# Low parts of 40 first-layer weight tiles made by adding transfers instead of GpSimd subtractions

## The reference, cut to what matters

```
h = rms_norm(x, norm_g)
q, k, v, gate = split(h @ w_in, 4)          # w_in is 2048 x 8192
q, k = partial_rope(q), partial_rope(k)     # 16 heads of 128
w = softmax(q1 k1) - lam * softmax(q2 k2)   # 8 pairs
o = rms_norm(w @ v, subln_g) * 0.8          # then o * silu(gate)
x = x + o @ w_out                           # w_out is 2048 x 2048
```

## Time and profile before

| | |
|---|---|
| median of 3 runs | 2815.59 us (2815.26 to 2817.22) |
| the profiled execution: its time, as the profile gives it | 2815.378 us |
| its span | 2815.4 us |
| PE busy | 2783.0 us, 99% |
| DVE, ACT, POOL busy | 1270.5, 996.7, 1170.6 us |
| DMA, mean rate | 88 GB/s |

### The profile page before, as it was taken

One profiled execution on the slowest core, in us unless ns is written; L12 is line 12 of the kernel. 1 busy time (PEld: TensorE's weight loads), 2 busy tenths in 40 slices (PEclk: granted clock), 3 DMA queues, 4 the chain that ended last, 5 costly groups with the idle time before them and its releaser, 6 DMA issues.

```text
span 2815.4 us, 41127 instructions
## 1 busy us (share of the span) xinstructions
PE 2783.0 (99%) x16886; PEld 2422.6 (86%) x16886; DVE 1270.5 (45%) x2182; ACT 996.7 (35%) x1466; POOL 1170.6 (42%) x895
## 2 busy tenths in 40 slices
PE   8999999999999999999999999999999999999997
PEld 8999999999999999777877778888788877887776
DVE  6333333334343358343434352744434334455646
ACT  5323232222323245344233354542323333234444
POOL 3343334334343434333434337444444334445443
PEclk9999999999999999999999999999999999999999
DMA  5122222222222222222222234222222222222221
GB/s 194 64 88 76 90 76 76 90 76 76 90 76 76 91 69 90 90 76 75 83 82 75 90 112 150 90 75 90 90 83 82 90 91 75 90 83 90 90 90 76
DMA packets 37115, 247.53 MB, mean 88 GB/s; under 512 B 4112, under 2 KB 4416, under 8 KB 8640
## 3 DMA queue, kind: packets, MB, share of 16 engines
q1 hardware_dynamic: 34992, 239.37, 24.0%
q10 hardware_dynamic: 1936, 5.53, 0.5%
HBM read 240.69 MB, written 4.19 MB: 87 GB/s over the span
## 4 chain that ended last, share of the span: by engine, by line
PE 91%; DVE 4%; ACT 2%; DMA 1%; POOL 1%; DVEq 1%; issue 0%; ACTq 0%; SPq 0%
PE pj L337 20%; PE pj L344 20%; PE pj L341 20%; PE pj L400 3%; PE pj L404 3%; PE pj L402 3%; PE pj L1184 2%; PE pj L1186 2%; PE pj L1185 2%; PE pa L586 1%; PE pa L549 1%; PE pa L1087 1%; POOL wl L2426 1%; DMA raw<-in_stream 1%; PE pj L1099 1%; PE pa L1523 1%
## 5 line engine op out<-in xcount | busy, mean ns | idle before, releaser
L2426 POOL TENSOR_TENSOR wl<-raw,wh 128x512 fp32r<-128x512 f32 x872 | 1158.9, 1360 | 1613.2 <-ACT wh L279 1613.2
L337 PE MATMUL pj<-xh,wh 128*128 128x264 f32 (+2 forms) x3728 | 1080.4, 336 | 2.9 <-POOL wl L2426 1.4
L341 PE MATMUL pj<-xl,wh 128*128 128x264 f32 (+2 forms) x3728 | 1044.7, 326 | 0.0
L344 PE MATMUL pj<-xh,wl 128*128 128x264 f32 (+2 forms) x3712 | 1040.9, 327 | 0.0
L279 ACT ACTIVATE wh<-raw 128x2048 fp32r<-128x2048 f32 x219 | 419.3, 1914 | 944.2 <-PE pj L344 594.8
L337 PEld LDWEIGHTS pj<-xh,wh 128*128 128x128 f32 x3728 | 633.8, 188 | 74.4 <-issue 15.2
L341 PEld LDWEIGHTS pj<-xl,wh 128*128 128x128 f32 x3728 | 631.0, 188 | 62.0 <-issue 7.2
L344 PEld LDWEIGHTS pj<-xh,wl 128*128 128x128 f32 x3712 | 628.0, 188 | 59.4
L429 DVE TENSOR_TENSOR acc<-pj,acc 128x528 f32<-128x528 f32 (+1 forms) x192 | 134.2, 699 | 126.7 <-PE pj L404 125.6
L400 PE MATMUL pj<-oh,wh 128*128 128x264 f32 (+1 forms) x608 | 167.2, 326 | 3.5 <-DVE ol L931 1.5
L404 PE MATMUL pj<-oh,wl 128*128 128x264 f32 (+1 forms) x608 | 165.1, 323 | 0.0
(11 more groups left out here) (331 smaller groups left out, 2804.5 us busy)
## 6 DMA issues: line engine op xcount, KB each, us to landing
raw<-in_stream SPq DMA_DIRECT2D x219, 1024.0 KB, 4.8
acc<-in_x SPq DMA_DIRECT2D x8, 528.0 KB, 8.8
raw<-in_stream SPq DMA_DIRECT2D x8, 256.0 KB, 8.1
arena<-in_mem ACTq DMA_DIRECT2D x2, 1024.0 KB, 6.1
out_y<-arena SPq DMA_DIRECT2D x4, 512.0 KB, 2.9
out_y<-arena ACTq DMA_DIRECT2D x3, 512.0 KB, 4.5
out_y<-arena SPq DMA_DIRECT2D x1, 384.0 KB, 4.4
cos<-in_cos_a SPq DMA_DIRECT2D x1, 264.0 KB, 11.9
```

What stands on the lines that cost most here:

```text
L337: pe.matmul(pj[:, pu, b, 0:m], whk, xh[:, k, a:a + m], start=(k == 0), stop=False)
L341: ins = pe.matmul(pj[:, pu, b, 0:m], whk, xl[:, k, a:a + m], start=False, stop=(both and k == KD - 1))
L344: ins = pe.matmul(pj[:, pu, b, 0:m], wlk, xh[:, k, a:a + m], start=False, stop=(k == KD - 1))
L2426: pool.tensor_tensor(wl[:, j, at], raw[:, j, at], wh[:, j, at].bitcast(F32), ALU.subtract).then_inc(s_part if c < LO_PARTS - 1 else s_lo, 1)
```

## The change

For the 40 tiles 22 to 61, ACT writes wl = -round(raw) with one more instruction of the full 128 x 2048 just ahead of the one that writes wh. POOL then issues two transfers of 128 x 1024 float32 (512 KB each) which read the tile in HBM once more and add it to what stands in `wl`, so that raw - round(raw) is left there. POOL waits for each transfer, raises `s_part` twice after the first and once after the second, and then waits for `s_hi` and raises `s_lo`. The other tiles are as before.

```
+LO_BY_DMA = range(22, 62)
 ...
             act.wait_ge(s_out, used + 1)
+            if t in LO_BY_DMA:
+                act.activation(wl[:, par_t, :], raw[:, par_t, :], ACT.Copy, scale=-1.0).then_inc(s_neg, 1)
             act.activation(wh[:, par_t, :], raw[:, par_t, :], ACT.Copy).then_inc(s_hi, 1)
 ...
+            def lo_by_dma(t, j):
+                n = t - LO_BY_DMA[0]
+                pool.drain()
+                pool.wait_ge(s_neg, n + 1)
+                half = WCOLS // 2
+                for c in range(2):
+                    at = slice(c * half, (c + 1) * half)
+                    pool.dma_start(wl[:, j, at], dram["stream"][t][:, at], accum_op=ALU.add).then_inc(s_low[c], 16)
+                pool.wait_ge(s_low[0], 16 * (n + 1))
+                pool.sem_inc(s_part, 2)
+                pool.wait_ge(s_low[1], 16 * (n + 1))
+                pool.sem_inc(s_part, 1)
+                pool.wait_ge(s_hi, t + 1)
+                pool.sem_inc(s_lo, 1)
 ...
+                    elif pair * 2 + j in LO_BY_DMA:
+                        lo_by_dma(pair * 2 + j, j)
```

More of the change, by code:

```diff
@@ L153, in build @@
         s_out = sem("s_out")
+        s_neg = sem("s_neg")
+        s_low = [sem("s_low0"), sem("s_low1")]
         s_evac = sem("s_evac")
```

## The result

The changed kernel takes 2820.67 us (median of 14 runs, 2819.75 to 2824.03), the kernel before 2816.11 us (14 runs, 2815.26 to 2817.32). The ratio is 1.0016, 95% interval 1.0009 to 1.0024: 4.6 us slower, clear of its own interval and still inside the 0.2% that the prediction called no change. The forecast was 2818.9 us, range 2815 to 2848.

A forecast was written before the change was run, and what follows sets the result against it. TensorE, busy for 516.18 of 516.50 us in pairs 2 to 5, was taken as the limit. Removed work 0 to 0.3 us, delayed exponentials 3.3, other terms 0: 2818.9 us against the median, range 2815 to 2848.

The forecast's parts named there:

- What bounds the kernel; removed work is worth 0 to 0.3 us.: Pairs 2 to 5: TensorE's pace is the limit, so removing POOL's 210 us of subtractions gives back at most 0.3 us.
- The high part 1.92 us later costs nothing.: ACT's high part comes 1.92 us later behind the negated copy; tile 31 still has 8 us to spare, cost nothing.
- The exponentials behind the pair.: Stages 3 and 4, pairs 2 to 5: the longer ACT pair delays exponentials, PE waits; 3.3 us taken.
- The widening of the margin in pairs 4 and 5: Narrower slack there may widen to pair 2's once POOL's subtractions are gone: 3.0 instead of 3.5 us, 3.3 taken.
- The second sigmoid is covered.: A pair's second sigmoid starts 1.92 us later; VectorE's 2.45 us wait for PE behind it covers this, cost nothing.
- rival 3: VectorE, freed of POOL's interference, swallows the ACT delay, leaving 0 to -0.3 us: 2815.3 us; chance 0.06.
- The adding transfers land 8.7 us after the copy, cost 0.: Both halves land 8.7 us after the negated copy; w_out tiles allow 9.5 and 10.1 us, so no wait.
- a cover of 0.8 us: At the first w_out tile, the margin between the expected landing at 8.7 us and the 9.5 us allowed.
- Rival 1: Additions land late at the 8 w_out tiles, from 9.5 us on: 2824.5, 2836 or 2849 us; chance 0.27.
- Rival 2: Above 11.7 us per landing, transfers bound every tile: up to 128 us more, 2944 us; chance 0.11, shared with another rival.
- The total: 2815.4 us of the profiled execution plus 3.3 gives 2818.7; against the median 2818.9 us, +0.12%, counted as no change.

The follow-up runs named there:

- E4: The change for 24 tiles only, without the w_out tiles and those ahead of exponentials in stages 3 and 4: 2816.25 us, ratio 1.0000 to the kernel before.
- E10: Changed kernel with one 1 MB adding transfer per tile, and in stages 3 and 4 the negated copy behind the first following exponential: 2816.07 us, ratio 0.9998.
- E1: Changed kernel without adding transfers: ScalarE makes the negated copy, GpSimd's four subtractions then overwrite it as before: 2819.53 us, ratio 1.0012.
- E3: The change for 32 tiles, without the two per pair of heads ahead of exponentials (stages 3 and 4): 2818.26 us, ratio 1.0007.
- E5: Changed kernel with plain transfers in place of the adding ones, so wl holds the whole weight: 2818.79 us, ratio 1.0011.
- E6: Changed kernel with one adding transfer of 1 MB per tile in place of two of 512 KB: 2819.48 us, ratio 1.0013.
- E8: Changed kernel where SP loads the next tile without waiting for the low part, so beside the adding transfers: 2841.15 us, ratio 1.0088.
- E7: Changed kernel where ScalarE writes the high part first and the negated copy second: 2832.43 us, ratio 1.0059.

## Why the prediction was right, and where it was not

- *What bounds the kernel; removed work is worth 0 to 0.3 us.* Right. 134 us less of POOL and 16 us less of VectorE moved nothing (E4 for 24 tiles, E10 for all 40). The cap of 0.3 us from the earlier trace rows held in every experiment: none was measurably faster.
- *The high part 1.92 us later costs nothing.* Right: the list of waits for pairs 2 to 5 has none of PE for it.
- *The exponentials behind the pair.* Right in place and mechanism (E1, E3, E10), 3.3 us predicted, 2.8 measured. In stage 4 the term was 2.7, measured 2.2. In stage 3 I had 0.8 and found 0.6: a wait of 0.11 us was worked out from rows that left 0.12 us over. Both have the same error: I took the second instruction of the pair as 1.9 us behind the first one's end, and the following exponential's start after that. But ScalarE's instructions overlap by 0.1 us, as 352.24, 354.06 and 355.86 above show: the next one starts 3.62 us after the pair does, not 3.83. With 3.62 the working gives waits of 0.41 us in stage 4 of pair 2 and 0.26 in stage 3 of pair 5, where 0.52 and 0.39 were measured, so a further 0.1 us at each place goes the other way; its cause is open. The widening of the margin in pairs 4 and 5, for which I had taken 0.2 us off, did not come: pair 5's stage 3 is longer by 0.39 us in E1 and by 0.39 in the changed kernel.
- *The second sigmoid is covered.* Right. VectorE's steps there even became shorter, as rival 3 had it; its timeline after, which answers to the earlier trace rows:

```profile
390.92 0.71 DVE L927 TENSOR_TENSOR arena<-arena 128x528 f32<-128x528 f32 x1
391.73 1.33 DVE L936 TENSOR_TENSOR ol<-arena,oh 128x528 fp32r<-128x528 f32 x2
```

  0.71 us in place of 1.64 for the same instruction: beside POOL's subtractions it had taken more than twice as long. The Trainium skill's rule ("SBUF — State Buffer", Who interferes with whom), that two SBUF inputs on VectorE contend with a GpSimd instruction that reads SBUF, agrees. Against the kernel before it is worth nothing: no tile of E4 is shorter. But it keeps the added copy from costing more, since with the subtractions left in place (E1) PE waits 0.13 us per pair for a VectorE instruction beside them, and without them (E5) it does not.
- *The adding transfers land 8.7 us after the copy, cost 0.* This step failed: the landing was mis-sized (9.2 us in the median), and a cover of 0.8 us was held against one number where the landings scatter. Term by term: the lead, from the end of the copy to the first packet, is 1.9 us and not the 0.9 read off SP's load. POOL needs 0.3 us to begin and 0.87 for the first issue, and the first packet comes 0.7 after that. The moving is 7.0 us, as predicted, but by luck: I had doubled the 3.5 us of a single load (its row shows 24 busy slices and not 26, but its packets do take 3.5, from 393.33 to 396.81 us), and a single adding transfer moves in 6.1 (E6). The two halves take 0.9 longer than one transfer, where I had put the second issue at 0.5. A packet takes 1.9 times as long as a plain one (E5), so doubling was nearly right as such. With 0.3 us for the landing, 1.9 + 6.1 + 0.9 + 0.3 makes the measured 9.2 us. Against 9.5 and 10.1 us of room even that median fits; but tiles scatter from 8.4 to 11.5 us. Part of the scatter is the load of the next tile, which falls beside the transfers when the tile before was late: the six tiles that had most of it beside them (30, 31, 44, 45, 50, 51) landed after 9.9 to 11.5 us, and E8 shows what a load costs. But tiles with no load packet beside them scatter too, up to 10.4 us, and why was not found. Five of the eight w_out tiles were late, 3.0 us in all.
- *Rival 1* was therefore partly real: the forecast's case and the mild end of rival 1 came together. Its price was wrong in form: (D - 9.5) + (D - 10.1) adds two waits of which the first gives the second its room (E7). It also left out the slow clock after waits of 2.5 us and more (E7, E8). *Rival 2* was not met, but barely: from the copy to s_lo POOL took at most 11.7 us, one tile of TensorE's, and in E8, where it took longer, proj tiles were late. The two pages of the Trainium skill that the prediction named gave 6.8 us for the landing, an estimate; the rule that an add halves the rate agrees with 328 against 174 ns, while the landing measured 9.2 us, and 8.3 with a single transfer.
- *The total*, 2818.9 against 2820.67: 0.5 us too much for the exponentials, 3.0 us missing at w_out, and the median of the kernel before 0.5 us higher in the larger set of runs make 2821.9. The 1.2 us left over are most likely the 3.0, which is one execution: E3 has the same transfers at w_out, its trace has 2.1 us there and its median is 2.0 us above the kernel before. That landings scatter enough from one execution to the next to explain the rest was not measured. The forecast came within 1.8 us partly because the too large term and the missing one are of opposite sign. The prediction's sum also set the span of the profiled execution, 2815.4 us, beside a median of device times. In the runs that list both, the time is 1.8 us longer than the span in the median and never less than 1.7, so that execution was probably the one of 2817.22 us, slower than the median and not 0.2 below it. The forecast does not change by this, since it is the median plus 3.3.

## What to carry to other kernels

When one engine is busy for all but 0.3 us of a stretch, work taken from the others cannot pay; what such a change can do is make that engine wait, so price each new step by its place in its engine's queue and by the margin behind it, not by its busy time: eight copies, 15 us of work, cost 2.8 us at one place in ScalarE's queue and nothing three instructions later. A margin has to be held against the spread of a latency, not against its middle, and the load that shares the queue belongs to that spread. Two waits behind one another on one engine are not to be added when the second one's work runs on during the first.

## What the runs showed of the hardware

- Two POOL-issued adding transfers of 512 KB hold POOL for 1.75 us together, 0.87 us the first, and move 4 KB packets in 328 ns, against 174 ns for a plain one from the same queue (E5). One transfer of 1 MB holds POOL for 0.87 us in the median, no longer than the first of half the size, and lands 0.9 us sooner than two halves (E6).
- A load of 1 MB that falls beside them delays their landing by 2.5 us (E8: 11.4 against 8.9 us from the first issue).
- ScalarE instructions of 1.92 us that follow one another start 1.82 us apart (352.24 and 354.06 us in the changed kernel).
- A VectorE instruction with two SBUF inputs of 32 x 528 took 0.69 us alone and 1.45 us beside POOL's subtractions (E5, E1).
- TensorE's granted clock was 0.50, the 1.2 GHz level, for 3.4 us after idle stretches of 2.48 to 3.75 us in the middle of dense work, six times in E7 and E8, at a cost of about 1.6 us each. Two stretches of 2.35 and 2.84 us in E8, and all of 1.3 us and less in pairs 2 to 5, left it at 1.00.
